# The second block's norms without GpSimd, one gated layer scaled on evacuation, and three first unit pairs run by k tiles

## What is computed

```python
def rms_norm_2(x, g):
    x32 = x.astype(jnp.float32)
    y = x32 * lax.rsqrt(jnp.mean(x32 * x32, axis=-1, keepdims=True) + EPS)
    return (y * g.astype(jnp.float32)).astype(x.dtype)

def swiglu(u, w_gate, w_up, w_down):
    return (jax.nn.silu(u @ w_gate) * (u @ w_up)) @ w_down

def sublayer(h, i, fn, resid_w):
    shift, scale, gate = mod[:, i, 0, None, :], mod[:, i, 1, None, :], mod[:, i, 2, None, :]
    u = rms_norm_2(h, norm_pre[l, i]) * (1.0 + scale) + shift
    return h + resid_w * gate * rms_norm_2(fn(u), norm_post[l, i])

h = sublayer(h, 0, swiglu_1, 0.5)
h = sublayer(h, 1, token_mixer, 1.0)
h = sublayer(h, 2, swiglu_2, 0.5)
```

## Time and profile before

| | us |
|---|---|
| median of 3 runs | 1531.34 (1526.86 to 1535.13) |
| the profiled execution's own time | 1526.11 |
| its span, first to last instruction | 1524.4 |
| TensorE busy | 1406.8 (92%) |
| VectorE busy | 972.4 (64%) |
| ScalarE busy | 595.2 (39%) |
| GpSimd busy | 111.7 (7%) |
| mean granted TensorE clock | 0.968 of full |

### The profile page before, as it was taken

One profiled execution on the slowest core, in us unless ns is written; L12 is line 12 of the kernel. 1 busy time (PEld: TensorE's weight loads), 2 busy tenths in 40 slices (PEclk: granted clock), 3 DMA queues, 4 the chain that ended last, 5 costly groups with the idle time before them and its releaser, 6 DMA issues.

```text
span 1524.4 us, 29341 instructions
## 1 busy us (share of the span) xinstructions
PE 1406.8 (92%) x11884; PEld 1353.8 (89%) x11884; DVE 972.4 (64%) x1227; ACT 595.2 (39%) x564; POOL 111.7 (7%) x132
## 2 busy tenths in 40 slices
PE   5989898998999989899899899998899988699997
PEld 4988788998999989799899899997798878599997
DVE  3474455788765785578876587765675336585544
ACT  2344123433424424454343434333334454434432
POOL 2020000000000100000000111102120000200001
PEclk9999888999999999999999999999899999799998
DMA  5443204556775533455678388894473234275671
GB/s 166 138 117 105 83 2 138 165 186 201 207 217 169 180 114 111 140 165 178 208 207 245 128 271 275 266 259 141 151 240 129 88 134 138 77 258 190 187 195 59
DMA packets 263068, 252.52 MB, mean 166 GB/s; under 512 B 4681, under 2 KB 250572, under 8 KB 262996
## 3 DMA queue, kind: packets, MB, share of 16 engines
q1 hardware_dynamic: 251808, 212.37, 45.3%
q0 software_dynamic: 10992, 39.06, 7.5%
q10 hardware_dynamic: 196, 0.06, 0.0%
HBM read 250.42 MB, written 1.05 MB: 165 GB/s over the span
## 4 chain that ended last, share of the span: by engine, by line
PE 77%; DVE 11%; ACT 5%; issue 5%; DMA 1%; POOL 1%; DVEq 0%; SPq 0%; ACTq 0%; POOLq 0%
PE ps L1696 66%; ACT w_hi L414 3%; DVE w_lo L891 3%; PE ps L1738 1%; DVE proj L911 1%; DMA raw<-in_fox_w_in 1%; PE ps L1877 1%; PE ps L1812 1%; POOL proj L1610 1%; PE ps L2094 1%; PE ps L1862 1%; DVE proj L1393 1%; PE ps L1856 1%; DMA raw<-in_ffn_w_down 1%; PE ps L1667 1%
## 5 line engine op out<-in xcount | busy, mean ns | idle before, releaser
L1696 PE MATMUL ps<-x_hi,w_hi 128*128 128x256 f32 (+2 forms) x2304 | 672.4, 292 | 35.8 <-DVE x_lo L1009 11.9
L1696 PE MATMUL ps<-x_hi,w_lo 128*128 128x256 f32 (+2 forms) x2304 | 662.0, 287 | 0.0
L1696 PE MATMUL ps<-x_lo,w_hi 128*128 128x256 f32 (+2 forms) x2304 | 661.8, 287 | 0.0
L891 DVE TENSOR_TENSOR w_lo<-raw,w_hi 128x2048 fp32r<-128x2048 f32 (+1 forms) x188 | 458.0, 2436 | 218.6 <-ACT w_hi L414 218.0
L414 ACT ACTIVATE w_hi<-raw 128x2048 fp32r<-128x2048 f32 (+1 forms) x188 | 380.2, 2022 | 490.9 <-PE ps L1696 466.3
L1696 PEld LDWEIGHTS ps<-x_hi,w_hi 128*128 128x128 f32 x2304 | 441.7, 192 | 46.2 <-issue 38.1
L1696 PEld LDWEIGHTS ps<-x_hi,w_lo 128*128 128x128 f32 x2304 | 441.8, 192 | 0.0
L1696 PEld LDWEIGHTS ps<-x_lo,w_hi 128*128 128x128 f32 x2304 | 441.4, 192 | 0.3
L1696 PE MATMUL ps<-g_hi,w_hi 128*128 128x256 f32 (+2 forms) x768 | 218.3, 284 | 8.2 <-DVE g_lo L1557 3.0
L1696 PE MATMUL ps<-g_hi,w_lo 128*128 128x256 f32 (+2 forms) x768 | 217.4, 283 | 0.0
L1696 PE MATMUL ps<-g_lo,w_hi 128*128 128x256 f32 (+2 forms) x768 | 216.7, 282 | 0.0
(11 more groups left out here) (283 smaller groups left out, 1126.3 us busy)
## 6 DMA issues: line engine op xcount, KB each, us to landing
raw<-in_ffn_w_gate SPq DMA_DIRECT2D x44, 1024.0 KB, 5.3
raw<-in_ffn_w_up SPq DMA_DIRECT2D x44, 1024.0 KB, 5.3
raw<-in_ffn_w_down SPq DMA_DIRECT2D x32, 1408.0 KB, 6.9
v_tok<-in_w_ada POOLq DMA_DIRECT2D x72, 512.0 KB, 4.4
raw<-in_w_in SPq DMA_DIRECT2D x20, 1024.0 KB, 5.2
raw<-in_fox_w_in SPq DMA_DIRECT2D x16, 1024.0 KB, 5.8
raw<-in_hgrn_w_in SPq DMA_DIRECT2D x16, 1024.0 KB, 5.4
raw<-in_fox_w_out SPq DMA_DIRECT2D x4, 1024.0 KB, 4.8
```

The source lines that it names most:

```text
L891: V.tensor_tensor(w_lo[s][:, 0:size], raw[s][:, 0:size], w_hi[s][:, 0:size].bitcast(F32), ALU.subtract).then_inc(lo_ready, 1)
L1696: ins = T_.matmul(dst, w[:, kt, m * P:(m + 1) * P], x[:, kt, 0:T], start=(kt == 0 and i == 0), stop=(kt == kts - 1 and i == 2))
```

## The change

- `norm_pair` and GpSimd's `pair_sums` go. TensorE's sums of norms 4 to 9 take 8 float32 matmuls instead of 4. For the norms after a layer (5, 7, 9), ScalarE squares each unit straight from PSUM in its `evac` (`tile_squares`), and VectorE, after it, empties the bank with the gain already multiplied in (`gained_out`). For norm 4 ScalarE squares `h2` one k tile at a time, when `ffn1_down`'s loop is through.
- TensorE's sums of the first six k tiles (`tile_sums(.., 0, 6)`) stand inside the last pair of the layer before, between its units (`between`), or, for `mix_out`, inside its last unit (`mid`); the last two stand behind the layer.
- `post` works on two k tiles per instruction, without the gain.
- The put-off split for s = 1 is made in two halves (`first_half_hi`, `second_half_hi` and their `_lo`).
- In the first pair of `glu1_up`, `mix_in` and `glu2_up` TensorE runs both units k tile by k tile (`outer_pair`): for k tiles 0 to 4 both units, for 5 to 7 unit 0 alone, then unit 1's k tiles 5 to 7.
- `glu2`: `x_hi` and `x_lo` are made from `h2` times the gain, without `rstd` and without the shift. Two more columns of `x` hold the shift, so its 1056 matmuls have 258 columns. VectorE multiplies by `rstd` when it empties the banks and copies the shift's product out; Silu takes it as its bias. Norm 8's sum of squares stands inside the first pair, behind unit 0.
- `mod`'s columns 18 to 24 are read in the last pair of `ffn1_up`.

```diff
+            def first_half_hi(name):
+                pair = GEMMS[name]["first"] // 2
+                act.wait_ge(raw_landed[1], pair * 16 + 16)
+                act.wait_ge(unit_done, pair * 2 + 2)
+                nc.scalar.activation(w_hi[1][:, 0:UNIT // 2], raw[1][:, 0:UNIT // 2], ACT.Copy).then_inc(half_hi, 1)
...
+            def tile_squares(width):
+
+                def evac(it, s, pair):
+                    if s == 2:
+                        return
+                    read_wait(pair, s)
+                    nc.scalar.activation(sq[:, bass.ds(it * (2 * width) + width * s, width), 0:SEQ], ps[:, 2 * s:2 * s + width, 0:SEQ],
+                                         ACT.Square).then_inc(tile_sq, 1)
...
+            def glu2():
+                def evac(it, s, pair):
+                    if s == 0:
+                        act.wait_ge(banks_free[0], pair + 2)
+                        for m in range(2):
+                            ins = nc.scalar.activation(gated[:, m, 0:SEQ], conv[:, m, 0:SEQ], ACT.Silu, bias=bias_gate[:, m:m + 1])
+                        ins.then_inc(silu_done, 1)
...
+            last_down = GEMMS["ffn1_down"]["first"]
+            for k in range(KD):
+                evacuated(act, last_down + k)
+                if k == KD - 1:
+                    first_half_hi("glu1_up")
+                nc.scalar.activation(sq[:, k, 0:SEQ], h2[:, k], ACT.Square).then_inc(tile_sq, 1)
+            inverse_rms(4, SEQ)
+            second_half_hi()
...
+            for g in range(4):
+                act.wait_ge(h_updated, 4 + g + 1)
+                for k in range(2 * g, 2 * g + 2):
+                    ins = nc.scalar.activation(x_hi[:, k, 0:SEQ], h2[:, k], ACT.Copy, scale=mod_a[:, 2, k:k + 1])
+                ins.then_inc(x_hi_ready, 1)
+                nc.scalar.activation(sq[:, 2 * g:2 * g + 2, 0:SEQ], h2[:, 2 * g:2 * g + 2], ACT.Square).then_inc(norm_sq, 1)
+            inverse_rms(8, SEQ)
+            glu2()
...
+                def scale(g):
+                    V.tensor_tensor(xn[:, 2 * g:2 * g + 2, 0:SEQ], y_raw[:, 2 * g:2 * g + 2, :], rstd_pair_2, ALU.mult).then_inc(post_scaled, 1)
+
+                def add(g):
+                    dve.wait_ge(post_scaled, 4 * i + g + 1)
+                    V.tensor_tensor(h2[:, 2 * g:2 * g + 2], h2[:, 2 * g:2 * g + 2], xn[:, 2 * g:2 * g + 2, 0:SEQ], ALU.add).then_inc(h_updated, 1)
...
+                    if s < 2:
                         read_wait(pair, s)
+                        dst, bias = ((conv, bias_gate), (up, bias_up))[s]
+                        dve.wait_ge((silu_done, hidden_done)[s], it + 22)
+                        V.tensor_tensor(dst[:, :, 0:SEQ], ps[:, 2 * s:2 * s + 2, 0:SEQ], rstd_pair_2, ALU.mult)
+                        V.tensor_copy(bias.unsqueeze(2), ps[:, 2 * s:2 * s + 2, SEQ:SEQ + 1]).then_inc(banks_free[s], 1)
+                    else:
+                        dve.wait_ge(banks_free[1], pair + 2)
+                        dve.wait_ge(silu_done, it + (22 + 1))
+                        for m in range(2):
+                            ins = V.scalar_tensor_tensor(out=hidden_f[:, m, 0:SEQ], in0=up[:, m, 0:SEQ], scalar=bias_up[:, m:m + 1],
+                                                         in1=gated[:, m, 0:SEQ], op0=ALU.add, op1=ALU.mult)
...
-            def pair_sums(n):
-
-                for g in range(4):
-                    pool.wait_ge(norm_sq, 4 * n + g + 1)
-                    G.tensor_tensor(sq[:, 2 * g, 0:SEQ], sq[:, 2 * g, 0:SEQ], sq[:, 2 * g + 1, 0:SEQ], ALU.add).then_inc(norm_pair, 1)
...
+                        for kt in range(KD):
+                            for sm, v in xw(kt, 0):
+                                pe.wait_ge(sm, v)
+                            tile_products(kt, 0)
+                            if kt == 0:
+                                pe.wait_ge(half_lo, outer[0])
+                            if kt == KD // 2:
+                                pe.wait_ge(lo_ready, pair * 2 + 4)
+                            if kt < OUTER_KT:
+                                tile_products(kt, 1)
+                        if outer[1]:
+                            outer[1]()
+                        for kt in range(OUTER_KT, KD):
+                            tile_products(kt, 1)
...
+            gemm("ffn1_down", from_hidden(1), gh, gl, L - UNUSED, ada="ffn1_down", sums=(1, 4), between=lambda: tile_sums("ffn1_down", 0, 6))
+            tile_sums("ffn1_down", 6, KD)
+            gemm("glu1_up", from_norm(4), xh, xl, SEQ, ada="glu1_up", sums=(1, 11), outer=(1, None))
...
+            gemm("glu2_up", from_norm(6), xh, xl, SEQ + 2, ada="glu2_up", sums=(1, 5), outer=(3, lambda: norm_sum(5, SEQ)))
```

287 lines of the change are left out of this document (180 added, 107 removed).

## The result

The changed kernel takes **1557.35 us**, median of 4 runs (1551.87 to 1565.77), against 1531.03 for the kernel before on the same chip: **1.018 of the time**, 95% interval 1.012 to 1.023. The forecast was 1550, range 1540 to 1560, so the sign and the range held, and the forecast was some 7 us too low. The profiled execution took 1551.87 (span 1550.2, granted clock 0.971), 25.8 more than that of before.

A forecast was written before the change was run, and what follows sets the result against it. TensorE, busy 92% of the span, was taken as the bound. Terms 6.1 - 0.7 - 2.9 + 12.2 + 3.4 + 0.7 + 0.2 gave +19.0 us on 1526.1, so 1545; as a median 1550 us, range 1540 to 1560.

The forecast's parts named there:

- First changeover: From `ffn1_down` to `glu1_up` (norm 4): later sums and start, slow clock and a wait put the second pair 6.1 us later.
- Second: Changeover into `mix_in` (norms 5, 6): TensorE starts 2.9 us earlier, the first pair costs 2.2 more, 0.7 us earlier in all.
- Third: Changeover into `glu2_up` (norms 7, 8): TensorE starts 11.1 us earlier, of which 2.9 are left at the second pair.
- `glu2_up`: Inside this layer, the largest term: 12.2 us in four pairs with modulation, 3.4 in six plain turns, 0.7 in the last pair.
- ring with modulation: `glu2_up`'s dependent chain between VectorE and ScalarE in turns with `ada_half`: 14.8 us a turn, 12.2 us lost over four pairs.
- its rival, that ScalarE's order doesn't bind: In `glu2`, Silu and split fit under TensorE's other unit, so the kernel is not slower: 1529; chance 0.08.
- plain ring: `glu2_up`'s turns without `ada_half`, closing over TensorE: 11.93 us against 11.36, six times 0.57, 3.4 us.
- The last pair's wait: Last pair of `glu2_up`: its longer split adds 0.7 us.
- End: Behind the last layer (norm 9): sums cost 2.6, savings give it back, transposes waiting for pairs add 0.2 us.
- rival two: The clock doesn't fall at the starts since the sums are nearer, 2.3 us less three times: 1543; chance 0.10.
- rival three: Straight code of first and last pairs lets TensorE wait for instructions, 1 us at some eight places: 1558; chance 0.10.
- rival four: Changing PSUM bank every three matmuls keeps the three first pairs at half clock, +20 us: 1570; chance 0.03.

The follow-up runs named there:

- sums_behind: The changed kernel with norm 4's six sums moved from ahead of `ffn1_down`'s last unit to behind it: 1553.02 us, 1.0121 of before.
- outer2: The changed kernel with both units sharing 2 k tiles instead of 5 in the three first pairs: 1552.52 us, 1.0118 of before.
- sums_r: The changed kernel with squares of norms 4 to 9 rounded to fp32r and summed in one matmul a k tile: 1547.05 us, 1.0114 of before.
- glu2_old: The changed kernel with the last gated layer's scaling on evacuation undone (256 columns, Silu straight from PSUM): 1538.52 us, 1.005 of before.
- silu_late: The changed kernel with ScalarE's Silu in `glu2` moved behind both splits of the turn: 1539.06 us, 1.0046 of before.
- noouter: The changed kernel with the three first pairs run unit by unit again, half splits kept: 1558.9 us, 1.0189 of before.
- before_r: The kernel before with GpSimd's pair sums written rounded (fp32r) and summed by TensorE with rounded ones: 1529.84 us, 0.9978 of before.
- kept: The changed kernel without the last gated layer's scaling, norm 4's sums behind `ffn1_down`'s last unit, 2 shared k tiles, float32 sums: 1528.04 us, 0.9976 of before.
- best_a: The changed kernel without the last gated layer's scaling, norm 4's sums behind `ffn1_down`'s last unit, 2 shared k tiles, rounded sums: 1520.74 us, 0.9924 of before.

## Why the prediction was right, and where it was short

**First changeover: +6.1 forecast, +7.1 measured.** The wait for the square ahead of the last unit was forecast 2.3 and is 2.37, the sums 2.6 and 2.86. TensorE started 5.0 later in place of 4.6, lost 2.3 to the clock as forecast, and waited 2.90 for `w_lo` in place of 2.6. sums_behind and outer2 show two of the causes by themselves, 4.0 and 2.1 us (the latter from the two sums behind the layer on). One reading under this term was wrong. I took what the clock costs to lie under waits for `x_lo` in the kernel before, but inside that pair it had no such waits to speak of and lost as much to the clock, in 27 matmuls against 24. The sum came out because I had added up the new pair in full and taken the old one from its rows.

**Second: -0.7 forecast, +1.4 measured. This step failed.** The stage alone couldn't say so, as it moves by 5 us; its rows do. I had costed only the last two of norm 6's sums at half clock, 1.7 us, and let the others run beside the squares. At up to 0.43 a record all sixteen take 6.47, while ScalarE's four squares are through 3.6 us before `ln_ms` can start:

```profile
1071.14 1.23 ACT L782 ACTIVATE proj<-h 128x512 f32<-128x512 f32 x2 [0.57 <-DVE h L1480]
1075.92 0.47 ACT L467 ACTIVATE ln_ms<-ps,small 128x256 f32<-128x256 f32 x1 [3.55 <-PE ps L1884]
```

The earlier trace rows had the number: four records in 2.08 us at that very place. Doubling the count of sums made them the limit: in all seven traces with these float32 sums `ln_ms` waits for TensorE, 2.4 to 3.8 us, and in sums_r 0.89. How much they cost hangs on the clock. They took 6.4 to 6.7 us in four of the seven traces and 5.3 to 5.4 in the others, where the clock rose inside them:

```profile
1077.55 5.32 PE L1868 MATMUL ps<-proj,const_f_sb 128*128 128x256 f32 x16 [3.97 <-ACT proj L780]
```

That row is glu2_old's, whose code there is the changed kernel's. TensorE started 1.6 earlier and not 2.9, and the pair then cost 3.0 more and not 2.2.

**Third: -2.9 forecast, +0.4 measured in the stage.** The terms themselves held. From the start of `mix_out`'s second unit to that of `glu2_up` it is 31.8 us (1315.18 less 1283.39) against 41.3, and 15 matmuls in it took 1.4 us longer at half clock: 10.9 us without them (forecast 11.1). Norm 8's sums take 3.6 (3.5), the table load and the splits stand behind `rstd` as said, and without the clock 1.9 us are left. The rest is a term that my sum had not at all: ahead of it the clock fell twice where it had not, or not as long, 2.3 us together. 1.4 of it is at `mix_out`'s second unit (the last section). The other 0.9 is at the branches' output projections: behind a wait of 5.3 us in both kernels the clock stayed low for another 3.3 us before the change and for 5.2 after it.

**`glu2_up`: +12.2, +3.4 and +0.7 forecast; +12.35 and +5.9 measured.** The ring with modulation was forecast 14.8 and is 14.83 (the terms as I had written them add up to 14.7), and its rival, that ScalarE's order doesn't bind, is refuted by silu_late. The plain ring was forecast 11.93 and is 12.2:

```profile
1407.25 2.29 DVE L942 TENSOR_TENSOR w_lo<-raw,w_hi 128x2048 fp32r<-128x2048 f32 x1 [2.78 <-ACT w_hi L417]
...
1419.48 2.29 DVE L942 TENSOR_TENSOR w_lo<-raw,w_hi 128x2048 fp32r<-128x2048 f32 x1 [2.78 <-ACT w_hi L417]
```

From `w_lo`'s start to TensorE's (1409.79) are 2.54 us where I took 2.25: I used about the instruction's length and forgot the hand-over. The last pair's wait adds 2.34 against 0.77, for which I had 0.7.

**End: +0.2 forecast, 0 measured.** The rivals: the clock did fall at each start (rival two); the instruction queue moved 58 packets for 55 and no wait at the straight code is in the list (three); the changed kernel's first pairs, which change PSUM bank every three matmuls, ran 22 to 24 matmuls at 0.21 us and the rest at 0.12, so the whole pair at half clock of rival four did not come. The Trainium skill ("TensorE: Matmul & The Clock Gate", section "A second HAM failure mode: psum-queue depth-cycling") tells of a kernel that goes round its PSUM banks, idles shortly between groups of matmuls, and whose clock swings between its levels. That behaviour was not seen here, and a whole pair at half clock is more than the section says.

In sum +19.0 was forecast against +25.8 measured, and +27.3 without the 1.5 that the untouched work ahead gained by chance. Of the 8.3 us between 19.0 and 27.3, 1.3 are norm 6's sums and 0.8 the pair behind them, 2.3 the clock around `mix_out`, 1.8 the plain turns and the last pair, 1.0 the third changeover and 1.0 the first.

So the mechanism and the largest term were right. That the range held is in part luck: the bounds of the sum itself ended at 1556, below the measured 1557.35, and the range went on to 1560 for the sake of rival three, which didn't come about.

## What to carry to other kernels

When work moves from the engine that empties a bank to another, write down the ring of hand-overs for one turn with durations, and look at what stands between the links in each engine's list. Here one instruction in front of a split that did not need it made a chain of two engines the bound, at 2.5 us a turn with modulation, while VectorE was busy 73% of the time and ScalarE 35%. Moving sums to a faster engine pays only when that engine's time for them at the clock it will have is below what feeds it; and work that starts earlier gives its time back if the next link needs the same late number. Before reordering work to hide waits, look whether the trace shows waits inside it: here it showed them at the starts alone.

## What the hardware showed that I had not expected

The granted clock falls behind some waits of 1.9 to 3.1 us and not behind others, at places with the same code. Behind the wait ahead of norm 4's sums (2.37 us each time) the changed kernel kept 1.00 and noouter had 0.50, over the same stretch of 3.4 us:

```profile
844.30:847.70 3.40, 3.40 (x18) 3.09 (x19) 1.97 (x1) 1.79 (x6) 0.00 (x0) 1.00 0.44 156
```

```profile
847.30:850.70 3.40, 3.40 (x10) 2.64 (x9) 1.59 (x1) 1.42 (x5) 0.00 (x0) 0.50 0.46 155
```

The twelve records took 2.86 and 4.54 us. At the second unit of `mix_out` the kernel before waited 2.96 us and went on at full clock. before_r waited 2.97 at the same place and didn't, nor did the changed one behind 3.13. The first matmul behind the wait shows it, 0.38 us long at full clock and 0.58 at half (before, before_r, changed):

```profile
1275.40 0.38 PE L1696 MATMUL ps<-g_hi,w_hi 128*128 128x256 f32 x1 [2.96 <-DVE g_lo L1557]
```

```profile
1277.98 0.58 PE L1697 MATMUL ps<-g_hi,w_hi 128*128 128x256 f32 x1 [2.97 <-DVE g_lo L1558]
```

```profile
1283.39 0.58 PE L1808 MATMUL ps<-g_hi,w_hi 128*128 128x256 f32 x1 [3.13 <-DVE g_lo L1674]
```

At the second unit of `glu1_down` before_r lost the clock right behind a wait of 1.91 us. So the wait's length alone doesn't decide it; what else does is open. Such a fall cost 1.4 to 1.7 us here where the clock came back within 3.4 us. At `mix_out` in before_r, outer2, noouter, kept and best_a it stayed low for 6.8 us, and the stretch from there to norm 7's first sums was 1.1 to 1.3 us longer than the changed kernel's in the last four of them. A part of the spread between runs of one kernel (14 us in the changed one) may come from them. In this trace the changed kernel kept its clock ahead of norm 4's sums, where four of the other five kernels with that wait did not, which fits with a median above it; that was seen and not tested.
